# Forget-gate rows of an attention kernel: fp32 products with two rows a head, or one rounded pass with four

## The reference

```
log_f = jax.nn.log_sigmoid((d_f + fox_b_f[l]).astype(jnp.float32))
cum = lax.cumsum(log_f, axis=1)
o_d = causal_block_attention(d_q, d_k, d_v, Dh ** -0.5, log_f_cum=cum)
# inside, for a block of 128 queries:
s = jnp.einsum('bqhd,bkhd->bhqk', q_blk, k).astype(jnp.float32) * scale
s = s + (args[2].transpose(0, 2, 1)[..., None] - cum_keys)     # cum[query] - cum[key]
s = jnp.where(causal, s, -jnp.inf)
p = jax.nn.softmax(s, axis=-1).astype(v.dtype)
```

## Time and profile before

| what | us |
|---|---|
| median of three runs | 2059.38 (2058.47 to 2060.08) |
| the profiled execution, its span | 2059.5 |
| PE busy | 1986.3 |
| DVE busy | 1116.4 |
| ACT busy | 834.1 |
| POOL busy | 363.5 |

### The profile page before, as it was taken

One profiled execution on the slowest core, in us unless ns is written; L12 is line 12 of the kernel. 1 busy time (PEld: TensorE's weight loads), 2 busy tenths in 40 slices (PEclk: granted clock), 3 DMA queues, 4 the chain that ended last, 5 costly groups with the idle time before them and its releaser, 6 DMA issues. The chain is left out here.

```text
span 2059.5 us, 27434 instructions
## 1 busy us (share of the span) xinstructions
PE 1986.3 (96%) x10484; PEld 1606.7 (78%) x10488; DVE 1116.4 (54%) x2037; ACT 834.1 (40%) x1736; POOL 363.5 (18%) x345
## 2 busy tenths in 40 slices
PE   8999999999999999999999999799999999999997
PEld 7776588888887877568888888688788887886786
DVE  5789644423434489835643543579765331525554
ACT  4445633312323244744321332453433334535532
POOL 1336700000000153740000000003030330004300
PEclk9999999999999999999999999999999999999999
DMA  6321023322323432013543533222225222341232
GB/s 193 96 80 52 1 80 105 103 92 92 102 103 76 117 106 78 12 43 112 193 144 102 174 106 110 87 87 92 72 78 159 76 69 93 96 139 42 82 123 82
DMA packets 177523, 198.27 MB, mean 96 GB/s; under 512 B 38755, under 2 KB 140786, under 8 KB 176882
## 3 DMA queue, kind: packets, MB, share of 16 engines
q1 hardware_dynamic: 177394, 196.53, 30.1%
HBM read 180.74 MB, written 11.55 MB: 93 GB/s over the span
## 5 line engine op out<-in xcount | busy, mean ns | idle before, releaser
L161 DVE TENSOR_TENSOR weight_pairs<-weight_ring,weight_pairs 128x1024 fp32r<-128x1024 f32 (+4 forms) x293 | 354.9, 1214 | 399.2 <-ACT weight_pairs L152 397.9
L182 PE MATMUL psum<-operand,weight_pairs 128*128 128x512 f32 x1320 | 526.8, 399 | 11.6 <-PEq L230 8.7
L152 ACT ACTIVATE weight_pairs<-weight_ring 128x1024 fp32r<-128x1024 f32 (+4 forms) x293 | 303.6, 1039 | 528.4 <-PE psum L184 513.9
L183 PE MATMUL psum<-operand,weight_pairs 128*128 128x512 f32 x1320 | 516.9, 392 | 0.0
L184 PE MATMUL psum<-operand,weight_pairs 128*128 128x512 f32 x1320 | 516.9, 392 | 0.0
L182 PEld LDWEIGHTS psum<-operand,weight_pairs 128*128 128x128 f32 x1320 | 249.0, 189 | 71.4 <-issue 19.4
L184 PEld LDWEIGHTS psum<-operand,weight_pairs 128*128 128x128 f32 x1320 | 248.6, 188 | 53.9
L183 PEld LDWEIGHTS psum<-operand,weight_pairs 128*128 128x128 f32 x1320 | 249.1, 189 | 50.7 <-issue 1.0
L904 POOL TENSOR_SCALAR probs<-probs,stats 128x128 f32<-128x128 f32 (+3 forms) x176 | 163.5, 944 | 226.6 <-DVE stats L806 225.2
L182 PE MATMUL psum<-weight_pairs,hidden 128*128 128x512 f32 x512 | 200.7, 392 | 0.0
L183 PE MATMUL psum<-weight_pairs,hidden 128*128 128x512 f32 x512 | 200.0, 391 | 0.0
(11 more groups left out here) (433 smaller groups left out, 2757.9 us busy)
## 6 DMA issues: line engine op xcount, KB each, us to landing
weight_ring<-in_w_in_dram SPq DMA_DIRECT2D x100, 512.0 KB, 3.5
weight_ring<-in_w_up_dram SPq DMA_DIRECT2D x64, 512.0 KB, 3.7
weight_ring<-in_w_down_dram SPq DMA_DIRECT2D x64, 512.0 KB, 3.6
weight_ring<-in_w_out_dram SPq DMA_DIRECT2D x24, 512.0 KB, 3.5
ada_rows<-in_ada_w_dram SPq DMA_DIRECT2D x24, 512.0 KB, 4.6
spilled<-v_t SPq DMA_DIRECT2D x22, 256.0 KB, 2.1
weight_ring<-in_w_in_dram SPq DMA_DIRECT2D x20, 256.0 KB, 2.8
weight_ring<-in_w_proj_a_dram SPq DMA_DIRECT2D x8, 512.0 KB, 3.4
```

The source lines that it names most:

```text
L152: act.activation(self.pairs[:, i % SPLIT_RING, 0, 0:n], self.buf[:, i % RING, 0:n], ACT.Copy).then_inc(self.rounded, 1)
L161: dve.tensor_tensor(self.pairs[:, i % SPLIT_RING, 1, 0:n], self.buf[:, i % RING, 0:n], self.pairs[:, i % SPLIT_RING, 0, 0:n].bitcast(F32), ...
L182: pe.matmul(out, lhs[0], rhs[0], start=start, stop=False)
L183: pe.matmul(out, lhs[0], rhs[1], start=False, stop=False)
```

## The change

The gate products take the rounded format. A rounded value would be too coarse for 8 cum, so each side gets four rows a head: the rounded high part of 8 cum, the rest, and two rows of ones for the other side's. `gates` becomes fp32r, and the two gate matmuls of a pair read `32 * h` to `32 * h + 4`. `gate_forms` gets eight columns (offset, factor on the rounded part, a column that is used on the way, factor on the sum; for each side), found in sixteen steps in place of four, at another place. ACT rounds 8 cum after the scan and writes both sides' first form; DVE adds the factor on the exact sum.

```
-    gate_forms = sb("gate_forms", [P, 4])
+    gate_forms = sb("gate_forms", [P, 8])
...
             dve.tensor_copy(ident_half[:], ident[:]).then_inc(halved, 1)
-            own = Chain(dve, formed)
-            own(dve.tensor_reduce(gate_forms[:, 1:2], ident[:, 0:97:32], AX_X, ALU.add))
-            own(dve.tensor_reduce(gate_forms[:, 3:4], ident[:, 1:98:32], AX_X, ALU.add))
-            own(dve.tensor_scalar(gate_forms[:, 0:1], gate_forms[:, 3:4], 8.0, None, ALU.mult))
-            own(dve.tensor_scalar(gate_forms[:, 2:3], gate_forms[:, 1:2], -8.0, None, ALU.mult))
...
             dve.tensor_copy(conv_cols[:], psum[:, 1, 64:160])
+            own = Chain(dve, formed)
+            for side in range(2):
+                one, first, second, scaled = (gate_forms[:, 4 * side + i:4 * side + i + 1] for i in range(4))
+                r = 2 * side
+                own(dve.tensor_reduce(first, ident[:, r:r + 97:32], AX_X, ALU.add))
+                own(dve.tensor_reduce(second, ident[:, r + 1:r + 98:32], AX_X, ALU.add))
+                own(dve.tensor_reduce(scaled, ident[:, 2 - r:2 - r + 97:32], AX_X, ALU.add))
+                own(dve.tensor_reduce(one, ident[:, 3 - r:3 - r + 97:32], AX_X, ALU.add))
+                own(dve.tensor_tensor(one, one, scaled, ALU.add))
+                own(dve.tensor_tensor(first, first, second, ALU.subtract))
+                own(dve.tensor_scalar(scaled, second, 8.0, None, ALU.mult))
+                if side:
+                    own(dve.tensor_scalar(first, first, -1.0, None, ALU.mult))
+                    own(dve.tensor_scalar(scaled, scaled, -1.0, None, ALU.mult))
             norm.low(dve, 2)
...
-                gates = sb("gates", [P, 2, S], mix)
+                gates = sb("gates", [P, 2, S], mix, F32R)
...
             act.activation(gate_work[:, 1, :], gate_work[:, 1, :], ACT.Ln).then_inc(gate_log, 1)
             yield
+            act.wait_ge(gate_summed, 1)
+            act.activation(gate_work[:, 0, :].bitcast(F32R), gate_work[:, 1, :], ACT.Copy, scale=8.0).then_inc(gate_high, 1)
+            act.wait_ge(gate_high, 1)
+            for i in range(2):
+                act.activation(gates[:, i, :], gate_work[:, 0, :], ACT.Identity, bias=gate_forms[:, 4 * i:4 * i + 1],
+                               scale=gate_forms[:, 4 * i + 1:4 * i + 2]).then_inc(gate_rows, 1)
             yield
...
-            own(dve.tensor_tensor_scan(gate_work[:, 1, :], gate_work[:, 2, :], gate_work[:, 0, :], 0.0,
-                                       ALU.mult, ALU.add))
+            dve.tensor_tensor_scan(gate_work[:, 1, :], gate_work[:, 2, :], gate_work[:, 0, :], 0.0,
+                                   ALU.mult, ALU.add).then_inc(gate_summed, 1)
+            yield
             for i in range(2):
-                own(dve.tensor_scalar(gates[:, i, :], gate_work[:, 1, :], gate_forms[:, 2 * i:2 * i + 1],
-                                      gate_forms[:, 2 * i + 1:2 * i + 2], ALU.mult, ALU.add))
+                dve.wait_ge(gate_rows, i + 1)
+                own(dve.scalar_tensor_tensor(out=gates[:, i, :], in0=gate_work[:, 1, :], scalar=gate_forms[:, 4 * i + 3:4 * i + 4],
+                                             in1=gates[:, i, :].bitcast(F32), op0=ALU.mult, op1=ALU.add))
             yield
...
-                              (gates[32 * h:32 * h + 2, 0, q], gates[32 * h:32 * h + 2, 1, 0:w])]
+                              (gates[32 * h:32 * h + 4, 0, q], gates[32 * h:32 * h + 4, 1, 0:w])]
```

More of the change, by code:

```diff
@@ L1582, in front @@
              "roped_dve permuted scored rectified weighed selected squared mean_ready root_ready dve_own scaled turned_rows "
-             "kr_stored high low repeated gates_turned gate_read gate_abs gate_exp gate_arg gate_log kr_permuted kr_sined "
+             "kr_stored high low repeated gates_turned gate_read gate_abs gate_exp gate_arg gate_log gate_summed gate_high gate_rows kr_permuted kr_sined "
              "q_permuted q_sined pool_own copied_bk")
@@ L1587, in front @@
      roped_pool, roped_dve, permuted, scored, rectified, weighed, selected, squared, mean_ready, root_ready, dve_own, scaled,
-     turned_rows, kr_stored, high, low, repeated, gates_turned, gate_read, gate_abs, gate_exp, gate_arg, gate_log,
+     turned_rows, kr_stored, high, low, repeated, gates_turned, gate_read, gate_abs, gate_exp, gate_arg, gate_log, gate_summed, gate_high, gate_rows,
      kr_permuted, kr_sined, q_permuted, q_sined, pool_own, copied_bk) = sems
```

## The result

The changed kernel took 2066.98 us (median of 5 executions, 2065.13 to 2068.42) against 2059.38 us: a ratio of 1.0032 (95% interval 1.0022 to 1.0043), 7.6 us slower. The forecast was 2059.7 with a range up to 2063.6, so the time lies 3.4 us above the range. Nine more executions in a later set had a median of 2066.35 us, a ratio of 1.0024 (1.0014 to 1.0034) to 25 of the kernel before (2060.8 us): 5.5 us slower.

The account below looks back on a forecast made before the run. The prediction took the tensor engine (PE), busy 96% of 2059.5 us, as the bound. Start 2.9, clock 1.6, front 1.2 and attention -5.4 made +0.3 us, a forecast of 2059.7 us, range 2056.4 to 2063.6.

Parts of the forecast that it names:

- the late product: At the start, PE's first product should start near 23.1 us, after a wait of 4.6 us.
- the half clock: Right behind PE's first product, the granted clock should read 0.50 in a stretch.
- the shorter group: In the attention, the stretch of the forget-gate group should be 20 to 20.8 us and not 23.1.
- PE's waits in the group: In the forget-gate group of the attention, PE's waits should be near 1.9 us.
- the shift of the attention: In each layer, the first exponentials that PE waits for should come 0.6 us later, measured from the front's end.
- The opening, +2.9: At the start, sixteen DVE steps of 0.183 us each delay PE's first product by 2.9 us (2.7 to 3.2).
- The clock, 1.6: Behind the wait before PE's first product, one stretch of 3.4 us at half speed costs 1.6 us (0 to 3.4).
- The front, 1.2: Where each layer's gate rows are formed, DVE's changed steps and wait cost 0.6 us a layer, 1.2 in all (0 to 3).
- The attention, -5.4: Forget-gate group: PE work falls 4.0 us a layer, waits grow by 1.3, so 2.7 a layer is kept, 5.4 in all.
- The third rival: In the attention the whole saving arrives, 4.4 us a layer, and the clock stays up: -4.7, 2054.7 us; chance 0.10.
- the product that is no faster: In the attention, the rounded gate product with four rows gains nothing: +5.7, 2065.1 us; chance 0.05.

Follow-up runs that it names:

- start_bridged: The changed kernel with 120 in place of 40 small matmuls on the identity before PE's first product; 2062.87 us, ratio 1.0008 to the kernel before.

## Why the prediction was wrong, step by step

The mechanisms named for the four terms all occurred; the sum failed on what they came to. Without the clock the forecast was 2.9 + 1.2 - 5.4 = -1.3 us, and the traces show about +0.4 (3.05 + 2.3 - 5.0): the front was put too low and the gain too high. The clock was one stretch behind the opening, 1.6 us, and no term stood for a fall anywhere else: up to 1290 us the two traces of the changed kernel are 6.6 and 5.4 us late, of which 1.6 and 2.2 went at half clock behind the opening and 4.5 and 2.9 at later falls. Of the signs that it named, the late product, the half clock and the shorter group came; PE's waits in the group (0.9 us for 1.9) and the shift of the attention (1.1 for 0.6) did not.

**The opening, +2.9: right.** 3.06 us by the trace, 0.19 a step; the first product 0.15 us from where it was put, the wait 4.77 for 4.6. The price of 75 ns a step that the prediction took from the Trainium skill's page "Vector Engine (DVE) Microarchitecture Reference", section "Rate slope and fixed cost", would have given an estimated 1.2; the row of the trace of before decided rightly.

**The clock, 1.6: the right mechanism behind the opening, nothing for falls elsewhere.** The prediction took one stretch of 3.4 us at half speed, half of it lost, and put two stretches at the end of its range. Both occurred: one in the profiled execution (1.6 us lost, as forecast), one twice as long, its first 2 us ahead of the product, in the next (2.2 lost). By the medians the start alone cost 5.4 us, 2.4 over its 3.05, and bridging the wait brought 3.5 (11 and 9 executions). Its sentence that the shift stays from there to the attention, because PE paces everything, missed the fall at 112 us.

**The front, 1.2: too small.** The traces give 1.1 and 1.2 us, 2.3 in all, the timed kernel 2.9. DVE's steps were priced well (1.53 for 1.44). Mis-sized was the wait for ACT, 0.63 for 0.3 a layer: three passes of 2.1 us together were put at 1.9, and so the rounding ended later (160.10 us in the changed kernel, 2.95 behind the scan's end, for 2.7). That the delay arrives in full at the attention was right.

**The attention, -5.4: nearly right by the trace (-5.0), from two errors that cancel.** The product saves less than said, 1.59 us a sweep and not 2.0. From 0.26 and 0.43 us the step is 0.20 fixed and 0.057 for each 128 keys. The earlier trace rows can be read as 0.21 fixed for a step and 0.21 for each 128 keys; the prediction split the 0.21 over the two passes and let half of it go with one of them. It did not go: the columns pass as fast as the earlier trace rows said, the fixed part is that of the step. And the waits grew by 0.3 us a layer, not by 1.3. That the two offset each other was luck. The timed kernel with the product alone gave 3.6.

**The sum.** With what the experiments measured one by one, start with its clock 5.4, front 2.9, product -3.6, it is +4.7 us; the changed kernel showed +7.6 (4.5 to 8.9) and +5.5 (2.9 to 7.0). No term had the wrong sign. By these measures start with clock, front and product were off the same way, by 0.9, 1.7 and 1.8 us (each median is uncertain by some 2 us), and the range ended below that. It moved only the gain and the clock: the bounds that the prediction itself gave for the front, 0 to 3, were not carried into it. Both of its upper ends at once (gain 3.6, clock 3.4) make 2063.4, so 2063.6 is not the range "without both ends at once" that it is called. The third rival's 4.4 a layer does not follow either: 2.4 a sweep is 4.8. The nearest rival, the product that is no faster (2065.1), came closest in time and is false: a time near a rival's is no proof of its mechanism.

**The reference.** The kernel before was taken as 2059.4 us from three executions; 89 later ones have 2060.9. And a reported time is 1.7 us over the span of its execution (2065.13 for 2063.4): the profiled execution of before, of 2059.5, was one of some 2061.2 and not one 0.1 over the median, as the prediction had it. Shifting the forecast by that 1.7 us would still leave the measured time above the range.

**What stays open.** At equal mean clock, 0.990, the changed kernel is 2064.7 us (4 executions) and the one before 2062.1 (39), 2.6 us apart, and the changed kernel's clock is 0.0024 lower on the mean. That split into work and clock is rough: the 1.1 us for each 0.001 come from falls of the kernel before, nearly all of them behind 1300 us in its two traces, while a stretch of 3.4 us behind the opening, 0.0008 of the mean, cost 1.6. Bridging the start gives back 3.5 of the 5.5 us, yet both traces of the changed kernel also fall at 112 us, behind waits of 1.94 and 1.79 us, where no other kernel's trace does; start_bridged has a longer wait there (timeline of PE, then the stretch):

```profile
111.15 0.46 PE L182 MATMUL psum<-weight_pairs,operand 128*128 128x420 f32 x1 [2.61 <-DVE weight_pairs L161]
```

```profile
111.15:118.00 6.85, 6.85 (x35) 6.50 (x36) 6.47 (x20) 1.06 (x1) 3.68 (x3) 1.00 0.42 101
```

and no half clock behind it. Whether the later start makes falls at 112 us more likely, or two executions met one by chance, these runs don't settle; the fall near 831 us is as open.

## What to carry to other kernels

Work on constants belongs where its engine waits anyway: the sixteen steps delay nothing at 2.3 us, and in front of the first product they cost 5.4 us, 2.4 of them by the clock. When a pass is thinned, split its measured time into a fixed part and a part by width from two widths, and ask which of them the thinner form keeps. And price the order on the engine that feeds the critical one (here ACT's rounding of weights), not the steps of the critical engine alone.

## What the runs showed of the hardware that was not expected

- Widening a tile of constants from 4 to 12 columns, without a further instruction, made the products on the hidden rows 2.9% slower (0.2333 for 0.2267 us apart, those on `operand` beside them unchanged) and the kernel 15.2 us slower; 8 columns did nothing of the kind. What the wider tile moves is the place of the tensors allocated behind it; which address matters was not tried.
- A wait of 4.77 us was followed by one stretch of half clock in two executions and by a doubled one in two others; a wait of 2.61 us at another place was followed by none, and waits of 1.94 and 1.79 us there by one.
- Of 5.9 us of gate steps left out in a stretch in which PE was busy for 22.5 of 23.1 us, 2.8 arrived.
